# Splitting four attention tiles and two output weight tiles ahead of a barrier in a hybrid decoder block

## The reference

```python
u = rms_norm(x, norm_mix_pre_w)
z, xbc, dt_raw, q, k, v, gate_ssd, gate_attn = _split(u @ w_in, IN_SIZES)
...
y_ssd  = gated_group_rms_norm(y, z, ssd_norm_w) @ ssd_w_out     # (1024, 2048) @ (2048, 1024)
y_attn = sliding_window_sink_attention(q, k, v, sinks) @ attn_w_out   # (1024, 1024) @ (1024, 1024)
merged = sigmoid(gate_ssd) * y_ssd + sigmoid(gate_attn) * y_attn
x = x + rms_norm(merged @ w_mix_out, norm_mix_post_w)
...      # then a gated ConvFFN
```

## Time and profile before

| | |
|---|---|
| median of 3 runs | 2165.63 us (2164.36 to 2166.37) |
| profiled execution | 2168.98 us, span 2167.4 us |
| TensorE busy | 2090.6 us, 96% |
| VectorE, ScalarE, GpSimd busy | 1307.5, 844.0, 598.4 us |
| mean granted TensorE clock | 0.984 |
| mixers' last transposes, SyncE's first issue of the late stage | 1101.83 us, 1106.80 us |

### The profile page before, as it was taken

The page is one execution under the profiler, slowest core; times in us unless marked ns, Lnnn a source line. Parts: engine busy times, 40 slices in busy tenths (PEclk is TensorE's granted clock), DMA queues, the critical chain, the costliest instruction groups (busy, mean ns, idle before and its releaser), DMA issues. The chain is left out here.

```text
span 2167.4 us, 29054 instructions
## 1 busy us (share of the span) xinstructions
PE 2090.6 (96%) x10218; PEld 1739.7 (80%) x10218; DVE 1307.5 (60%) x1824; ACT 844.0 (39%) x1589; POOL 598.4 (28%) x600
## 2 busy tenths in 40 slices
PE   7999999979999999999979999999999999999997
PEld 6888889967878778778758888887888888878885
DVE  6854552237767767777743344558887777752523
ACT  5332221024454444454443222434444443443432
POOL 1000011146576666565610000004222222100000
PEclk9999999989999999999989999999999999999998
DMA  6122241223443433443355434321222222355343
GB/s 225 62 90 97 87 166 69 84 85 129 119 125 117 124 114 124 124 131 97 95 175 179 141 134 145 122 94 72 88 87 71 75 87 87 138 161 195 112 151 88
DMA packets 131264, 252.73 MB, mean 117 GB/s; under 512 B 25264, under 2 KB 70448, under 8 KB 131152
## 3 DMA queue, kind: packets, MB, share of 16 engines
q1 hardware_dynamic: 85584, 174.98, 24.9%
q0 software_dynamic: 15360, 55.32, 7.5%
q10 hardware_dynamic: 30208, 20.98, 3.0%
HBM read 189.63 MB, written 61.60 MB: 116 GB/s over the span
## 5 line engine op out<-in xcount | busy, mean ns | idle before, releaser
L155 PE MATMUL ps_zg<-u_hi,g_hi 128*128 128x512 f32 x448 | 186.0, 415 | 0.0
L157 PE MATMUL ps_zg<-u_hi,g_lo 128*128 128x512 f32 x448 | 177.1, 395 | 0.0
L156 PE MATMUL ps_zg<-u_lo,g_hi 128*128 128x512 f32 x448 | 176.2, 393 | 0.0
L2057 DVE TENSOR_TENSOR lt_d_lo<-lt_w_raw,lt_d_hi 128x640 fp32r<-128x640 f32 (+1 forms) x64 | 57.1, 892 | 147.2 <-ACT lt_d_hi L1782 142.5
L973 POOL TENSOR_TENSOR mx_seg<-mx_seg,mx_cbm 128x1024 f32<-128x1024 f32 x32 | 76.0, 2376 | 161.3 <-DVE mx_cbm L1130 161.3
L155 PE MATMUL ps_zg<-z_w,u_hi 128*128 128x512 f32 x256 | 108.6, 424 | 7.1 <-DVE mx_silu L1155 6.9
L155 PE MATMUL lt_ps<-lt_h_hi,lt_w_hi 128*128 128x512 f32 x256 | 100.7, 393 | 14.8 <-DVE lt_h_lo L2095 13.6
L157 PE MATMUL ps_zg<-z_w,u_lo 128*128 128x512 f32 x256 | 102.3, 400 | 0.0
L156 PE MATMUL ps_zg<-z_w,u_hi 128*128 128x512 f32 x256 | 101.8, 398 | 0.0
L1782 ACT ACTIVATE lt_d_hi<-lt_w_raw 128x640 fp32r<-128x640 f32 (+1 forms) x64 | 50.6, 791 | 130.5 <-PE lt_ps L157 119.6
L1656 POOL TENSOR_TENSOR lt_t_f<-lt_w_raw 128x512 f32<-128x512 f32 x21 | 29.1, 1385 | 261.7 <-DVE lt_t_lo L1985 260.2
(11 more groups left out here) (390 smaller groups left out, 6229.8 us busy)
## 6 DMA issues: line engine op xcount, KB each, us to landing
lt_w_raw<-in_w_up SPq DMA_DIRECT2D x44, 512.0 KB, 4.5
mx_a_row<-acs_s SPq DMA_DIRECT2D x32, 512.0 KB, 3.9
g_raw<-in_w_xbc SPq DMA_DIRECT2D x24, 512.0 KB, 3.2
lt_sig<-gate_s SPq DMA_DIRECT2D x24, 512.0 KB, 3.6
lt_w_raw<-in_w_down SPq DMA_DIRECT2D x32, 384.0 KB, 3.2
ff_s<-lt_fo SPq DMA_DIRECT2D x21, 512.0 KB, 5.0
tok_s<-fr_work POOLq DMA_DIRECT2D x20, 512.0 KB, 3.8
lt_w_raw<-in_w_down SPq DMA_DIRECT2D x32, 320.0 KB, 2.9
```

Source lines behind the costliest of these rows:

```text
L155: pe.matmul(dst, s_hi, m_hi, start=first, stop=False)
L156: pe.matmul(dst, s_hi, m_lo, start=False, stop=False)
L157: return pe.matmul(dst, s_lo, m_hi, start=False, stop=last)
L2057: dve.tensor_tensor(d_lo[:, m % 2, 0:n], w_raw[:, m % 2, 0:n], d_hi[:, m % 2, 0:n].bitcast(F32), ALU.subtract).then_inc(dw_lo_done, 1)
```

## The change

Sources 0 to 3 (the first four attention tiles) and the weight tiles of products 0 and 1 are loaded and split in the mixers instead of the late stage. SyncE loads the weight of product 0 at step 4 of the last group, and that of product 1 at step 6, into the slots of the gate weights, and the four sources behind the last z product at step 7. ScalarE and VectorE split the weight of product 1 in step 6 and that of product 0 in step 7; ScalarE copies the sources' high halves in step 7 and behind it, and GpSimd makes their low halves behind its last step. TensorE runs k = 0 to 3 of product 0 (24 matmuls) ahead of the barrier, between its last transposes and values, into the bank pair of z and the gates, and k = 0 to 3 of product 1 (24 matmuls) as its first work behind the barrier; k = 4 to 7 of both follow as before. The late stage loads and splits 20 sources and 22 weights. As sources 0 to 3 lie where halves of sources 12 to 15 will go, product 7 uses them first, signals that (`o_used`), and sources 12 to 15 are split after that; sources 8 to 11 are split during products 2 to 5. The halves of the mixing weights get places of their own (`m_places`), and two of the mixers' buffers move within `raw_pieces`.

```diff
+EARLY = 4
+BASE = 17408
...
+        hold("spare", [P, 672])
...
+        self.o_raw = nc.alloc_sbuf_tensor_at("o_raw", [P, EARLY, D], F32, offset=BASE + 104 * 1024)
+        self.out_hi = nc.alloc_sbuf_tensor_at("out_hi", [P, KT, P], F32R, offset=BASE + 81 * 1024 + 256)
+        self.out_lo = nc.alloc_sbuf_tensor_at("out_lo", [P, KT, P], F32R, offset=BASE + 124 * 1024)
...
-        return self.raw[:, q % 2, 0:2 * GW].rearrange("p (k n) -> p k n", n=GW)
+        return self.raw[:, q % 2, GW:3 * GW].rearrange("p (k n) -> p k n", n=GW)
+    def o_part(self, low, k):
+        return self.z_w[:, low, 2 * k:2 * k + 2].rearrange("p a n -> p (a n)")
...
-                    if c % 2 == 0 and not (last and c >= 4):
+                    if c % 2 == 0:
                         u = 4 * g + c // 2
+                        src = A["w_attn_out"][u + 2 - 2 * KT] if last and c >= 4 else A["w_gate"][u + 2]
                         sp.wait_ge(g_lo_done, u + 1)
-                        sp.dma_start(g_raw[:, (c // 2) % 2], A["w_gate"][u + 2]).then_inc(g_in[(c // 2) % 2], 16)
+                        sp.dma_start(g_raw[:, (c // 2) % 2], src).then_inc(g_in[(c // 2) % 2], 16)
+                    if last and c == NT - 1:
+                        sp.wait_ge(z_done, NG * NT)
+                        for j in range(2):
+                            sp.wait_ge(o_stored[j], 16 * EARLY * NT // 4)
+                        for k in range(EARLY):
+                            sp.dma_start(carry.o_raw[:, k], o_s[k]).then_inc(o_in[k], 16)
                     if c == 1 and not last:
                         sp.wait_ge(z_lo_done, 4 * g + KT)
                         for q in range(2):
...
+            def split_o(k):
+                pool.wait_ge(o_hi_done, k + 1)
+                pool.tensor_tensor(carry.o_part(1, k), carry.o_raw[:, k], carry.o_part(0, k).bitcast(F32),
+                                   ALU.subtract).then_inc(o_lo_done, 1)
...
+            for k in range(EARLY):
+                split_o(k)
...
+            def split_o(k):
+                if k == 0:
+                    act.wait_ge(z_done, NG * NT)
+                act.wait_ge(o_in[k], 16)
+                act.activation(carry.o_part(0, k), carry.o_raw[:, k], ACT.Copy).then_inc(o_hi_done, 1)
...
-                    if c % 2 == 1 and not (last and c == NT - 1):
+                    if c % 2 == 1:
                         act.wait_ge(gate_done, n)
                         split_gate((c // 2 + 1) % 2, 2 * g + (c // 2 + 1) // 2)
+                    if last and c == NT - 2:
+                        act.wait_ge(g_in[1], 16 * (KT + 1))
+                        act.activation(carry.out_hi[:], g_raw[:, 1], ACT.Copy).then_inc(out_w_hi_done, 1)
+                    if last and c == NT - 1:
+                        split_o(0)
...
+                    if last and c == NT - 1:
+                        split_o(1)
...
+            for k in range(2, EARLY):
+                split_o(k)
             outputs(NG - 1, NT - 1, False)
...
-                    if c % 2 == 1 and not (last and c == NT - 1):
+                    if c % 2 == 1:
                         split_gate((c // 2 + 1) % 2, 4 * g + c // 2 + 1)
+                    if last and c == NT - 2:
+                        dve.wait_ge(out_w_hi_done, 1)
+                        dve.tensor_tensor(carry.out_lo[:], g_raw[:, 1], carry.out_hi[:].bitcast(F32),
+                                          ALU.subtract).then_inc(out_w_lo_done, 1)
...
+            def merge(k):
+                pe.wait_ge(o_lo_done, k + 1)
+                if k == 0:
+                    pe.wait_ge(g_lo_done, 2 * KT + 1)
+                for h in range(2):
+                    if k == 0:
+                        pe.wait_ge(gate_out if h else z_used, NG * NT)
+                    cols = slice(h * HALF, (h + 1) * HALF)
+                    matmul3(pe, carry.ps[:, h], g_hi[:, 0, k], g_lo[:, 0, k], carry.o_part(0, k)[:, cols],
+                            carry.o_part(1, k)[:, cols], k == 0, False)
...
+            merge(0)
             values(NG - 1, NT - 1)
+            merge(1)
             turn_outputs(NG - 1, NT - 1, False)
...
+        out_w = (carry.g_hi[:, 0], carry.g_lo[:, 0]), (carry.out_hi[:], carry.out_lo[:])
+        m_places = ((80, 84), (120, 124), (128, 132), (136, 140)) + tuple((88 + 4 * k, 104 + 4 * k) for k in range(EARLY))
+        m_hi = [at(f"m_hi{k}", place[0], [P, D], F32R) for k, place in enumerate(m_places)]
+        m_lo = [at(f"m_lo{k}", place[1], [P, D], F32R) for k, place in enumerate(m_places)]
...
+            if n < EARLY:
+                return carry.o_part(0, n), carry.o_part(1, n)
+            if n // KT == 1:
+                return m_hi[n % KT][:], m_lo[n % KT][:]
+            return h_hi[:, n % KT], h_lo[:, n % KT]
+        def next_srcs(n):
+            if n < 2 or n == KT - 2:
+                return range(0)
+            if n < KT - 2:
+                return range(KT + n - 2, KT + n - 1)
+            return range(KT + EARLY, 2 * KT) if n == KT - 1 else range(KT + n, KT + n + 1)
+        def merge_bank(n):
+            return carry.ps[:].rearrange("p a n -> p (a n)") if n == 0 else ps[:, n % 2]
...
-                if n >= 2:
-                    sp.wait_ge(w_lo_done, n - 1)
+                if n >= 4:
+                    sp.wait_ge(w_lo_done, n - 3)
...
-                load_merge(n)
-            for n in range(2):
+                load_merge(n + 2)
                 load_sig(n)
             for n in range(2, MERGE):
                 if n >= 2 * KT:
                     load_mix(n - 2 * KT)
-                load_merge(n)
+                if n >= 4:
+                    load_merge(n)
                 load_sig(n)
             for j in range(2):
...
-            for n in range(MERGE):
-                if n >= 3:
-                    pool.wait_ge(s_lo_done, n - 2)
-                pool.dma_start(y_t[:, n % 3], o_s[n] if n < KT else y_s[n - KT]).then_inc(s_in[n % 3], 16)
+            for m in range(SRCS):
+                n = m + EARLY
+                if m >= 3:
+                    pool.wait_ge(s_lo_done, m - 2)
+                pool.dma_start(y_t[:, m % 3], o_s[n] if n < KT else y_s[n - KT]).then_inc(s_in[m % 3], 16)
...
-            split_merge(0)
-            split_src(0)
-            split_merge(1)
-            for n in range(1, KT):
+            for n in range(EARLY, KT):
                 split_src(n)
+            for n in range(2):
+                split_merge(n + 2)
             for n in range(2 * KT):
                 sigmoid(n)
-                split_src(KT + n)
-                act.wait_ge(merge_done, n + 1)
-                split_merge(n + 2)
+                if n == 2:
+                    act.wait_ge(merge_done, 2)
+                if n == KT - 1:
+                    act.wait_ge(o_used, 1)
+                for src in next_srcs(n):
+                    split_src(src)
+                if n >= 2:
+                    act.wait_ge(merge_done, n + 1)
+                    split_merge(n + 2)
             for n in range(2 * KT, MERGE - 1):
                 sigmoid(n)
...
-                    dve.tensor_tensor(merged[:, f], sig[:, j], ps[:, j], ALU.mult).then_inc(out_done, 1)
+                    dve.tensor_tensor(merged[:, f], sig[:, j], merge_bank(n), ALU.mult).then_inc(out_done, 1)
...
-            split_merge(0)
-            split_src(0)
-            split_merge(1)
-            for n in range(1, KT):
+            for n in range(EARLY, KT):
                 split_src(n)
+            for n in range(2):
+                split_merge(n + 2)
             for n in range(2 * KT):
-                split_src(KT + n)
+                for src in next_srcs(n):
+                    split_src(src)
                 gate(n)
-                split_merge(n + 2)
+                if n >= 2:
+                    split_merge(n + 2)
...
-                return matmul3(pe, ps[:, n % 2, h * HALF:(h + 1) * HALF], w_hi[:, n % 2, k], w_lo[:, n % 2, k],
+                weights = (out_w[n][0][:, k], out_w[n][1][:, k]) if n < 2 else (w_hi[:, n % 2, k], w_lo[:, n % 2, k])
+                return matmul3(pe, merge_bank(n)[:, h * HALF:(h + 1) * HALF], *weights,
                                hi[:, h * HALF:(h + 1) * HALF], lo[:, h * HALF:(h + 1) * HALF], k == 0, k == KT - 1)
-            for k in range(KT):
+            for k in range(EARLY):
+                for h in range(2):
+                    merge(1, k, h)
+            for k in range(EARLY, KT):
                 for n in range(2):
-                    if k == 0:
-                        pe.wait_ge(w_lo_done, n + 1)
                     if n == 0:
-                        pe.wait_ge(s_lo_done, k + 1)
+                        pe.wait_ge(s_lo_done, k - EARLY + 1)
                     for h in range(2):
                         last = merge(n, k, h)
                     if k == KT - 1:
                         last.then_inc(merge_done, 1)
             for n in range(2, MERGE - 1):
```

(45 more changed lines are left out.)

23 lines of the change are left out of this document (12 added, 11 removed).

## The result

The changed kernel took 2178.56 us (median of 4, 2174.37 to 2181.27) beside 2166.00 us for the kernel before: a ratio of 1.0055, 95% interval 1.0042 to 1.0068. In a second comparison, made later, it was 1.0026 (1.0016 to 1.0037), 2173.37 beside 2168.08 us. Both intervals lie above 1 and both ratios above the 0.2% that can be told, the second narrowly (its interval begins at 0.16%); the forecast was 2160.1 us and faster. The profiled execution took 2174.37 us, the shortest of its four, so its trace accounts for 5.4 us over the profiled execution of before.

What follows compares the result with a forecast made beforehand. TensorE was taken as the bound, busy 2090.6 of 2167.4 us, its longest wait 13.6 us at the barrier. Terms: +4.8 + 2.7 - 13.0 = -5.5 us, from median 2165.63 to 2160.1 us; range 2156.5 to 2165.2.

Steps and rivals of the forecast that it cites:

- Everything before step 6 and from product 2 on keeps its length: Front, earlier mixer steps and late stage from product 2: no change in time, so no term in the sum.
- Step 7 and the tail: Last mixer step up to the barrier: weight split, clock and merges cost 2.7 us, ends 1.4 and 4.5.
- 1.35 us by the split: Step 7, VectorE from L1130 to L1140: splitting a gate weight takes 3.81 us instead of 2.46.
- 0.8 us on merge(3): Tail: GpSimd contending with VectorE could delay merge(3), making the tail some 0.8 us longer, inside the ends.
- 0.5 + 0.5 + 0.4 in the sum: Tail: 0.5 us of merge(1) ahead of the last transposes, 0.5 for the clock, 0.4 for merge(3).
- 1.98 against 1.23 us: VectorE's split beside GpSimd's work against one alone; the forecast took 1.5 us for the split in step 6.
- Step 6: Last group, ahead of the barrier: late-landing product 1 weights delay z by 4.8 us, ends 3.4 and 7.1.
- Behind the barrier: Late stage's start: early products fill the wait, so product 2 starts 13.0 us earlier, ends 12.2 and 13.4.
- the dear case: Mixers cost more through later weights and clock falls: 6.5 + 4.3 - 12.5 = -1.7, 2163.9 us; chance 0.27.
- The change does do what it says behind the barrier: Against the rival that the 48 matmuls only fill a wait behind the barrier: +5 us, 2171; chance 0.04.
- The rival for slower: Clock falls in step 6 and stays low through the tail: +13, about 2178 us; chance 0.05.

Runs made afterwards that it cites:

- the kernels with gaps: Kernel before with only unused floats held between SBUF tiles (such as 672 or 16 in front of z_w); those with both g tiles off cost 0.36 to 0.47%.
- The early load: Weights of product 1 loaded in step 5 instead of step 6, against the changed kernel with u moved up 128 bytes: 2159.60 us, ratio 0.9970 to before.

## Why the prediction was wrong

- **"Everything before step 6 and from product 2 on keeps its length": the step that failed.** What lies ahead of step 6 cost 5.6 us in the profiled execution (6.9 of it in the front, less some scatter of the mixers), and the unused floats alone cost 8 to 10 by the ratios of the kernels with gaps. With u moved the changed kernel is level with before; with the old pace the outcome would have been no change and not a loss. Of the 5.5 us forecast as a gain, 4.8 went to the other terms: 0.3 in step 6, 3.6 in the tail and 0.9 behind the barrier. I had read the 672 floats and the new places in the diff as a matter of room and costed them at nothing, with no bound. Nothing in the trace of before could have given the price; but each wait-free stretch of 1458 instructions in 300 us is a reading that could have been named as what would show it.
- **Step 7 and the tail, 2.7 us (1.4 to 4.5): mis-sized.** It measured 6.3. The 1.35 us by the split were right (L1130 to L1140 of the kernel before, 3.81 us forecast, took 3.82). The contention of GpSimd with VectorE was named, and put at 0.8 us on merge(3). It fell on the softmax: 2.1 us by the maximum, so that TensorE stood 3.9 instead of 1.8 us. Behind that came seven microseconds at a clock of 0.52, and the stretch up to the barrier, with 0.5 + 0.5 + 0.4 in the sum, grew by 2.8. "SBUF — State Buffer" of the Trainium skill, section "SBUF: two separate sides", has this as an exclusive lock for a whole instruction, for operations of VectorE with two inputs in SBUF, and not as a shared bandwidth; the 128x4 maximum under a 2.34 us subtraction agrees with it, where the 1.98 against 1.23 us that I went by looked like a mere slowing.
- **Step 6, 4.8 us (3.4 to 7.1): right**, 5.1, by the mechanism given: landing 5.5 us, a stand of 3.2, half clock behind it. The early load took all of it away.
- **Behind the barrier, -13.0 (12.2 to 13.4): right in kind, a little large**, -12.1, just outside its ends. The 24 products ran at full clock, so they ended earlier than I had them, the stand for source 4 became 4.0 us and the clock fell there, not at the barrier; and source 4 was copied 7.34 us behind SyncE's first load instead of 6.80.
- **Rivals.** The mixers were dearer (11.4 ahead of the barrier; the dear case had 10.8) but with what came back behind the barrier, 12.1, that alone is no loss. The clock came back each time. The change does do what it says behind the barrier. The rival for slower was the wrong one: it put some 2178 us on a clock that does not come back, and that the first median was 2178.56 is chance. No case had a price for the placement.

## What to carry to other kernels

A hold, a gap or a moved tile is an edit that can have a price of its own: after any change of placement compare a full, wait-free window of TensorE (instructions in 300 us) far from the change, and try first to keep weight and streamed tiles of 128x512 products in fp32r a multiple of 256 bytes apart. Work put into the last steps ahead of a barrier should arrive a step early, and GpSimd's large subtractions should not lie beside operations of VectorE with two inputs in SBUF, however small, on the chain that ends last.

## What the runs showed of the hardware

- A 128x512 product of fp32r in the front, with weights g and streamed tile u, takes 227 ns from start to start where the two lie a multiple of 256 bytes apart in a partition (256, 512 and 768 modulo 1024 tried), 232.5 where they are 128 off such a multiple (384 and 896 modulo 1024) and 233.4 where they are 64 off. In the mixers, with weights u and streamed tile z, it is 229.5, 232.8 and, at 64 off, 229.7. The front's 128x392 products of u kept 179 ns in both kernels. "SBUF — State Buffer" of the Trainium skill, section "Operand start alignment", asks only for a multiple of the element size and says that its runs timed nothing; here the time differs by 2.4%.
- Under GpSimd subtractions of 128x1024 (2.3 to 2.6 us each), VectorE's 128x4 maximum took 2.30 instead of 0.16 us, a 128x512 product 2.73 instead of 0.69, and yn 2.79 instead of 0.75.
